# An encoder layer on one core: cached sample keys turned on VectorE in 32x32 squares, and half of the sample values' low parts on GpSimd

## What is computed

```
# FoX branch: 8 heads of 64, cache of 512 keys per sample plus its 16 new ones
k_all = concatenate([cache_fox_k, k], axis=1)      # v_all in the same way
s = einsum('bqhd,bkhd->bhqk', q, k_all) * scale + cq - ck   # masked
o = einsum('bhqk,bkhd->bqhd', softmax(s), v_all)
# memory branch: 4 heads of 128, cache of 256 keys per sample, no new ones
o = einsum('bhqm,bmhd->bqhd', softmax(einsum('bqhd,bmhd->bhqm', qm, mk) * scale), mv)
```

## Time and profile before

| | |
|---|---|
| median of 3 runs | 1926.86 us (1926.57 to 1928.02) |
| span of the profiled execution | 1926.4 us |
| instructions | 33099 |
| TensorE's granted clock | 2.4 GHz, full level in all slices |
| FoX samples (first to last score reduction) | 555.0 to 653.8 us |
| memory samples (the same) | 784.1 to 852.9 us |

### The profile page before, as it was taken

How to read it: one execution, slowest core, us unless ns; L and a number is a source line. 1 busy time by engine, 2 the same in 40 slices (tenths; PEclk the granted TensorE clock), 3 DMA queues, 4 the chain that set the end, 5 groups by cost and what they waited for, 6 DMA issues and landing times. The chain is left out here.

```text
span 1926.4 us, 33099 instructions
## 1 busy us (share of the span) xinstructions
PE 1903.4 (99%) x12655; PEld 1869.4 (97%) x12655; DVE 1222.8 (63%) x2293; ACT 842.7 (44%) x1672; POOL 516.6 (27%) x547
## 2 busy tenths in 40 slices
PE   9999999999999999999999999999999999999998
PEld 8999999999999999999999999999999999999997
DVE  6685545454557666554334467687777977777765
ACT  7454434353546544443223332344444544444445
POOL 1004324250612123000000004276544433333320
PEclk9999999999999999999999999999999999999999
DMA  6451312213266643444233222233333433333323
GB/s 197 114 134 50 94 47 66 83 35 94 55 231 206 203 137 99 146 154 131 64 104 93 70 88 72 94 100 91 122 89 92 123 91 88 88 88 88 89 93 99
DMA packets 243601, 202.40 MB, mean 105 GB/s; under 512 B 16750, under 2 KB 217966, under 8 KB 243317
## 3 DMA queue, kind: packets, MB, share of 16 engines
q1 hardware_dynamic: 243445, 200.29, 34.8%
HBM read 166.62 MB, written 33.64 MB: 104 GB/s over the span
## 5 line engine op out<-in xcount | busy, mean ns | idle before, releaser
L1654 PE MATMUL ps<-act_hi,w_hi 128*128 128x384 f32 x1128 | 386.9, 343 | 0.9 <-DVE w_lo L597 0.6
L1654 PE MATMUL ps<-act_hi,w_lo 128*128 128x384 f32 x1128 | 378.0, 335 | 0.0
L1654 PE MATMUL ps<-act_lo,w_hi 128*128 128x384 f32 x1128 | 377.6, 335 | 0.0
L597 DVE TENSOR_TENSOR w_lo<-w_raw,w_hi 128x512 fp32r<-128x512 f32 (+1 forms) x200 | 198.0, 990 | 122.3 <-ACT w_hi L579 121.7
L1638 PE MATMUL ps<-ffs_hi,w_hi 128*128 128x288 f32 x832 | 245.8, 295 | 1.0 <-DVE h L2646 0.6
L1638 PE MATMUL ps<-ffs_hi,w_lo 128*128 128x288 f32 x832 | 245.2, 295 | 0.0
L1638 PE MATMUL ps<-ffs_lo,w_hi 128*128 128x288 f32 x832 | 244.9, 294 | 0.0
L1623 PE MATMUL ps<-bp_hi,pw_hi 128*128 128x288 f32 x784 | 231.6, 295 | 0.2 <-DVE pw_lo L2601 0.2
L1623 PE MATMUL ps<-bp_lo,pw_hi 128*128 128x288 f32 x784 | 231.3, 295 | 0.0
L1623 PE MATMUL ps<-bp_hi,pw_lo 128*128 128x288 f32 x784 | 231.2, 295 | 0.0
L579 ACT ACTIVATE w_hi<-w_raw 128x512 fp32r<-128x512 f32 (+1 forms) x200 | 152.6, 763 | 164.5 <-PE ps L1638 119.4
(11 more groups left out here) (356 smaller groups left out, 4190.7 us busy)
## 6 DMA issues: line engine op xcount, KB each, us to landing
w_raw<-in_w_down_dram SPq DMA_DIRECT2D x112, 256.0 KB, 3.4
pair_raw<-in_w_up_dram SPq DMA_DIRECT2D x28, 1024.0 KB, 5.5
w_raw<-in_w_in_dram SPq DMA_DIRECT2D x44, 512.0 KB, 4.4
merged<-prod SPq DMA_DIRECT2D x48, 192.0 KB, 2.0
prev<-merged SPq DMA_DIRECT2D x48, 192.0 KB, 3.8
foxs_vraw<-in_cache_fox_v_dram SPq DMA_DIRECT2D x8, 1024.0 KB, 6.1
foxs_kraw<-in_cache_fox_k_dram SPq DMA_DIRECT2D x7, 1024.0 KB, 5.6
x_in<-in_x_prompt_dram SPq DMA_DIRECT2D x8, 512.0 KB, 4.5
```

The source lines that it names most:

```text
L597: nc.vector.tensor_tensor(W[c % 2][1][:, 0:kt, :], w_raw[c % 2][:, 0:kt, :], W[c % 2][0][:, 0:kt, :].bitcast(F32), ALU.subtract).then_inc( ...
L1654: last = nc.tensor.matmul(bank(b)[:, 0:width], W[k][a][:, t, :], moving[z][:, t, j * width:(j + 1) * width], start=(t == 0 and n == 0), st ...
```

## The change

- The cached keys are loaded by four DMAs for a sample (`send_keys`): each brings 128 channels of all positions to 32 partitions, in pieces of 512 bytes, so that the partition is the position within 32.
- PE's `turn_keys` is gone. DVE turns the keys in squares of 32x32 (`keys_turned`, STREAM_TRANSPOSE) from `kraw` to a new SBUF tensor `kt_raw`; ACT's high and DVE's low part read `kt_raw` in place of PSUM. The channels of a head then lie in another order over partitions and quarters, so the queries, the new keys and the memory queries are put in the same order: `qs_raw` and `ks_raw` are filled by four ACT instructions of 32 partitions where one of 128 was, their high and low parts are made once in `first`, and the memory queries come by four DMAs.
- The queries are put into `qpad` by eight casts of 32 partitions for a sample, where FoX had four of 64 and memory two of 128.
- In the FoX samples DVE makes the low part of the left half of the values only; POOL makes the right half (`values_low`).
- In step 2 the values' low part now stands before the second `keys_lo`.

```diff
-        sf = dict(kraw=tensor("foxs_kraw", [P, ST, 512], R_AT), kt=parts("foxs_kt", [P, 4, ST * P + NQ], R_AT + 8192),
...
+        sf = dict(kraw=tensor("foxs_kraw", [P, PAST // QUAD, P], R_AT), kt=parts("foxs_kt", [P, 4, ST * P + NQ], R_AT + 8192),
+                  kt_raw=tensor("foxs_kt_raw", [P, 4, ST * P + NQ], R_AT + 8192 + 16 * (ST * P + NQ)),
...
         def values_split(eng, c):
-            eng.wait_ge(sa["v_lo"], 2 * c if c <= NB else NB + c)
+            eng.wait_ge(sa["v_lo"], c)
+            reached(eng, "values_low", min(c, NB))
...
+            def send_keys(a, i):
+                for y in range(4):
+                    sp.dma_start(raw_keys(a, i)[quadrant(y), :, :], a.kd[i][:, :, y * P:(y + 1) * P]).then_inc(sa["k_in"], 16)
...
+            def values_low(i):
+                pool.wait_ge(sa["v_hi"], i + 1)
+                pool.wait_ge(sa["k_new"], min(i + 2, NB))
+                pool.wait_ge(sa["vn"], 3 * (i + 1))
+                half = slice(2 * P, 4 * P)
+                nc.gpsimd.tensor_tensor(sf["v"][1][:, :, half], sf["vraw"][:, :, half], sf["v"][0][:, :, half].bitcast(F32),
+                                        ALU.subtract).then_inc(st["values_low"].sem, 1)
+
+            new_keys(0)
+            new_values(0)
+            for i in range(NB):
+                if i + 1 < NB:
+                    new_keys(i + 1)
+                values_low(i)
+                if i + 1 < NB:
+                    new_values(i + 1)
...
-            def turn_keys(a, i, part):
-                c = a.base + i
...
-                    for t in range(a.tiles):
-                        last = nc.tensor.transpose(ps[:, j % 2, t * P:(t + 1) * P], raw[:, t, j * P:(j + 1) * P], ident[:])
-                    last.then_inc(sa["kt_over"], 1)
...
+            def keys_turned(a, i, part):
+                c = a.base + i
+                if part == 0:
+                    dve.wait_ge(sa["k_in"], 64 * (c + 1))
+                    if i:
+                        dve.wait_ge(sa["s_over"], c)
+                for j in (2 * part, 2 * part + 1):
+                    nc.vector.transpose(a.b["kt_raw"][:, j, 0:a.tiles * P],
+                                        raw_keys(a, i)[:, :, quadrant(j)]).then_inc(sa["kt_over"], 1)
+
             def keys_lo(a, i, part):
...
-                    nc.vector.tensor_tensor(a.b["kt"][1][:, j, 0:a.tiles * P], ps[:, j % 2, 0:a.tiles * P],
+                    nc.vector.tensor_tensor(a.b["kt"][1][:, j, 0:a.tiles * P], a.b["kt_raw"][:, j, 0:a.tiles * P],
                                             a.b["kt"][0][:, j, 0:a.tiles * P].bitcast(F32),
                                             ALU.subtract).then_inc(sa["kt_lo"], 1)
...
                 for x in range(2):
...
+                    for y in range(4):
+                        at_ = a.b["qpad"][x if a.new else 0][quadrant(y), :]
+                        new = a.q[x][quadrant(y), :, i * NQ:(i + 1) * NQ].bitcast(F32)
...
                 if part == 0:
                     dve.wait_ge(at_s["pv_over"], PAIRS + M_PAIRS * k)
+                    keys_turned(a, 0, 0)
+                    keys_turned(a, 0, 1)
                     keys_lo(a, 0, 0)
+                    if a.new:
+                        for n, (part, raw) in enumerate(((QS, qs_raw), (KS, ks_raw))):
+                            reached(dve, "new_hi", n + 1)
+                            nc.vector.tensor_tensor(part[1][:], raw[:], part[0][:].bitcast(F32),
+                                                    ALU.subtract).then_inc(st["new_lo"].sem, 1)
...
                 elif part == 1:
+                    if i + 1 < NB:
+                        keys_turned(a, i + 1, 0)
                     dve.wait_ge(sa["pt_hi"], c + 1)
...
                 elif part == 2:
+                    if i + 1 < NB:
+                        keys_turned(a, i + 1, 1)
                     if i and a.new and i + 1 < NB:
                         out_lo()
+                    dve.wait_ge(sa["v_hi"], c + 1)
+                    cs = slice(0, 2 * P if a.new else 4 * P)
+                    nc.vector.tensor_tensor(b["v"][1][:, :, cs], b["vraw"][:, :, cs], b["v"][0][:, :, cs].bitcast(F32),
+                                            ALU.subtract).then_inc(sa["v_lo"], 1)
                     if i + 1 < NB:
                         keys_lo(a, i + 1, 1)
```

More of the change, by code:

```diff
@@ L834, in fox @@
                     sp.wait_ge(at_s["s_over"], UNITS)
-                    sp.dma_start(raw_keys(samples[0], 0)[:], samples[0].kd[0]).then_inc(sa["k_in"], 16)
+                    send_keys(samples[0], 0)
                 if s == 18:
@@ L867, in mem_parts @@
                 values_split(sp, NB)
-                sp.dma_start(mqs_raw[:], mem_q[:, :, SEQ:T]).then_inc(me["in"], 16)
+                for h in range(MH):
+                    sp.dma_start(mqs_raw[quadrant(h), :, :],
+                                 mem_q[:, h, SEQ:T].rearrange("(j r) q -> r j q", r=QUAD)).then_inc(me["in"], 16)
             def mem(s):
@@ L1127, in _, with new_keys @@
             pool.wait_ge(at_s["o_stored"], 16 * BT)
-            for i in range(NB):
+            reached(pool, "new_lo", 2)
+            def new_keys(i):
                 if i:
@@ L1418, in values @@
                         for y in range(2):
-                            if y == 1 and a.new:
-                                pe.wait_ge(sa["v_lo"], 2 * c - 1 + g)
+                            if y == 1 and a.new and g == 0:
+                                pe.wait_ge(sa["v_lo"], c)
                             elif y == 1:
@@ L1547, in beside_pe @@
                     fox(*args)
-                elif what == "first":
-                    turn_keys(samples[args[0]], 0, args[1])
                 elif what == "sample":
@@ L2052, in beside_act @@
                     keys_hi(samples[args[0]], 0, args[1])
+                    if args == (0, 0):
+                        for part, raw in ((QS, qs_raw), (KS, ks_raw)):
+                            nc.scalar.activation(part[0][:], raw[:], ACT.Copy).then_inc(st["new_hi"].sem, 1)
                 elif what == "sample":
@@ L2140, in leave @@
                             act.wait_ge(po["tail"], BT)
-                        last = nc.scalar.activation(rest[0][:, s.i, :], src[:, LAST:TB], ACT.Copy, scale=scale)
+                        for y in range(4):
+                            last = nc.scalar.activation(rest[quadrant(s.i), y, :], src[quadrant(y), LAST:TB],
+                                                        ACT.Copy, scale=scale)
                     last.then_inc(ev_hi, 1)
@@ L2442, in queries @@
             def queries(a, i):
-                c, per = a.base + i, a.heads // 4
+                c = a.base + i
                 if i:
```

72 lines of the change are left out of this document (29 added, 43 removed).

## The result

The changed kernel takes 1977.8 us (median of four runs, 1976.0 to 1978.8), the kernel before 1927.0 in the runs beside it: ratio 1.0261, 95% interval 1.0249 to 1.0274, so 50.8 us slower. The forecast of 1961, with a range up to 1976, had the direction right and 17 us too little.

What follows compares the result with a forecast made beforehand. PE, 1% free, bounds the kernel; DVE's chain would become the bound. FoX samples 24.2, weight splits 2.4, start 3.0 + 0.7, memory samples 4.0: +34.3 on 1926.4, so 1961 us (main case, 0.50), range 1936 to 1976.

Steps and rivals of the forecast that it cites:

- TensorE's saving: 192 key transposes leave PE at 0.11 us each: 21.1 us in all, 1.76 per FoX sample, 0.88 per memory sample.
- The transposes: Four DVE STREAM_TRANSPOSE of 128x512 per FoX sample, taken at 0.60 us each, bounded by 0.3 and 1.2.
- The estimate of 1.24 us: Alternative time of one 128x512 VectorE transpose, four times the skill's 128x128 figure; would make the sum some 8 us longer.
- The casts held by GpSimd: FoX query casts on DVE wait for GpSimd's subtraction on the values' right half: 2.7 us per sample.
- VectorE's chain as a whole: DVE's serial steps in a FoX sample, from probabilities to second low key pair: 10.2 us, before GpSimd's 2.7 us hold.
- Memory samples: Seven memory samples lose 2.9 us, plus some 1.1 before their first scores: +4, bounds -7 and +8.
- rival C: FoX loop: main case with keys' four partial DMAs landing late, first transposes 1.6 us later six times: 1971 us; chance 0.13.
- Rivals A and B: FoX loop: A, DVE's chain keeps up, 1906 or 1916 us, chance 0.10; B, casts not held up, 1942 us, 0.22.
- The start: Ahead of the first FoX scores: DVE's added transposes, low parts, clears and casts make them 3.0 us later.
- The first interval: First to second FoX score reduction, without values products: 15.6 us by the same chain against 14.9, +0.7.
- Three weight splits: In three FoX samples a split leaves little idle before the probabilities, so transposes push the chain by 0.8 each: 2.4 us.
- The 1.14 us of the value part: FoX samples: DVE's value part, now ahead of the second low key pair, charged 1.14 us per sample.

Runs made afterwards that it cites:

- a_filled: Changed kernel with 50 identity transposes on TensorE ahead of each FoX sample's wait for the query casts; 1964.9 us, ratio 1.0195.
- before_delayed: Kernel before, with 12 unused VectorE reductions of 128x512 ahead of each FoX sample's query casts; 1990.4 us, ratio 1.0332.
- new_values_early: Changed kernel with the two small transfers of a FoX sample's new values issued ahead of its cached values' transfer; 1973.9 us, ratio 1.0243.
- a_values_last: Changed kernel with VectorE's value part behind the second low pair of the keys, in FoX and memory samples; 1974.6 us, ratio 1.0246.
- out_first: Changed kernel with the small low part of the previous sample's output ahead of the second pair of transposes on VectorE; 1973.3 us, ratio 1.0243.
- pool_casts: Changed kernel with VectorE's chain reordered, all values' low parts on VectorE, FoX query casts on GpSimd, new values' transfers first; 1946.2 us, ratio 1.0102.

## Why the prediction was wrong in size

**Right.** TensorE's saving, and that VectorE becomes the bound. The transposes: 0.60 taken, 0.62 measured. The estimate of 1.24 us that the prediction worked out from the Trainium skill (VectorE: DVE Perf Modes, "The three transpose paths") is twice what the rows show; no run here has a transpose of 128x128 or in bf16. The casts held by GpSimd: 2.7 us estimated, 2.3 measured as GpSimd's subtraction and 2.0 as the excess of the casts. VectorE's chain as a whole: the second low pair was forecast to end at T0+12.9, it ends at T0+13.2. That is luck in part: the first low pair is 1.0 us longer than forecast, and the casts with their hold 0.7 shorter. From the scores' end to the next turn 4.2, as forecast. Memory samples: +2.9 forecast for the seven intervals and +1.1 ahead of them, measured +3.7 and nothing. The +3.7 are that part's order, as the runs show. Keys' DMA: one wait of 0.70 us in the loop, so rival C was no part of it. Rivals A and B did not come about.

**The step that failed** is the one from this chain to the end of the scores: "does the first half of the scores, waits for the second pair, and ends the last quarter of the scores at T0+11.1", with GpSimd's hold T0+13.8. They end at T0+16.3. The prediction's own terms let TensorE wait 3.8 us ahead of the scores (T0+5.3 to T0+9.1) and 1.8 us inside them, and run as in the earlier trace rows all the same; but in the earlier trace rows it hardly idles, and the speed there is that of an engine that does not wait. The scores start at T0+11.1 and not T0+9.1, since the first low pair is 1.0 us longer, the casts are 0.7 shorter, and the scores are released by L2527, 1.7 us behind the casts. After 5.8 us of idle TensorE then runs at half level, 1.2 GHz, for nearly all the scores. That is worth 10 us in the six intervals and 2.4 in the start (`a_filled`), and `before_delayed` shows it without the change. The Trainium skill says as much (TensorE: Matmul & The Clock Gate, "HAM oscillation — how this bites in real kernels"): a wait for data inside a loop lets the clock fall anew on every turn of the loop. By it the forecast would have had half level in the rows that follow each of the long waits, and that is what the trace shows.

**A second term was left out.** The first low pair of the keys read PSUM before and reads two tiles of SBUF now. The earlier trace rows was applied to the casts alone. The Trainium skill (SBUF — State Buffer, "Who interferes with whom") puts it so that a VectorE instruction with two inputs in SBUF contends with a GpSimd instruction that reads SBUF, while one with at most one such input, outside the two-port modes, does not. The rows agree on each: the pair from SBUF takes 2.30, the one from PSUM 1.29, and the transposes beside a GpSimd subtraction 1.30. It is worth some 4 us: 4.0 as the sum of the five excesses, 3.9 in `new_values_early`, with the uncertainty said above.

**Smaller ones.** The start was put at +3.0 and came to +6.1: half level 2.4, and the keys' first transfer came 1.25 us late; what made up for part of that was not looked into. The first interval was put at 15.6 "by the same chain"; 18.0 less the values' 2.1 is 15.9, and 16.7 came. Three weight splits were to cost 0.8 each; the probabilities start at T0+2.77, T0+2.01 and T0+2.00 in those samples and at T0+1.86 in the others, 1.2 us in all and not 2.4. The 1.14 us of the value part ahead of the second pair were charged, but not on the path (`a_values_last`): at half level the scores reach their third quarter after the pair. In their place the release of the scores, by the small instruction behind the second transposes, is on it, 1.1 us per interval in the profiled run of `out_first`, which was 2.0 us faster than its median; at full level the second pair would hide it, which is argued from the rows and was not run. Against the 26.6 us forecast for the six intervals 39.4 came: 10 are the clock, and the rest, 2.8, is no more than what the third hold is worth; that it is this hold is argued. The range's upper end is not C with transposes at 1.2 us by the prediction's own terms: 1971 and 0.6 us for each of the two transposes on the chain, six times, are 1978. That this is near the measured time is chance, since neither late keys nor slow transposes came about.

What stays open: what decides between the two levels after 2 to 3 us of idle, and how the terms divide where they overlap; the single edits give back 12.9, 12.3, 7.3, 4.5, 3.9 and 3.2 us, of which the second and third remove the same hold, and the last lies mostly in the first interval and the memory samples.

## What to carry to other kernels

A forecast in which an engine that never waited gets a wait of several us must price what comes behind the wait at the low clock too: here a wait of 4 us or more cost its length and, on top, 1.3 to 2.5 us, because 2.9 to 3.0 us of scores took 4.3 to 5.5. When an operand moves from PSUM to SBUF, list again what GpSimd does at that moment: in these runs its help was free beside VectorE's transposes and its subtractions with one input in PSUM, and held its casts and its subtractions with two inputs in SBUF. Moving GpSimd's work in time moved the hold to the next such instruction, which may be the one that others wait for. The order counts by itself: the same work cost the memory samples 3.7 us in one order and nothing in another. And look for what releases a waiting engine by its semaphore, not by its size: 0.2 us of work decided when the scores start.

## What the runs showed of the hardware

Filling 5.5 us of idle with useless transposes made the program 12.9 us faster. Idle of up to 1.7 us was followed by FoX scores at full level in all kernels; after 1.85 us (`pool_casts`) they started at full level and fell to half from the seventh of 24 matmuls. After 2.0 to 3.0 us either level was seen (2.03, 2.70, 2.76 us: full; 2.31 us: full, then half; 2.53 us: half; 2.98 us: once half, once full), and from 3.35 us on half level, with three cases (3.94, 3.95, 4.02 us) in which the first two matmuls were still faster. These are pairs seen here, not a threshold. A STREAM_TRANSPOSE of 128x512 in f32 steps by 0.62 us and is not held by a GpSimd subtraction; a subtraction of 128x64 on VectorE (0.18 us) was held to 1.31.
